# A hybrid decoder trunk on one core: the last 128 tokens leave the dense U products and take gathered rows

## The chip, the cores and the metric

The kernel runs on one core of one Trainium2 chip. Its engines are TensorE (PE, with its weight loads PEld), VectorE (DVE), ScalarE (ACT), GpSimd (POOL) and SyncE (SP), which issues transfers. The metric is the device time of one launch in microseconds. Everything is computed in float32; a product of two float32 matrices is made of three TensorE passes on rounded parts: hi x hi, hi x lo and lo x hi, where lo = raw - hi.

## The reference

512 tokens of width 1024 go through two layers. A layer mixes tokens in three ways (stick-breaking attention, a short convolution, a trailing-window pool), gates and projects the result, and then calls the retrieval feed-forward, which is what the change is about:

```python
q = xn @ w_query                       # 8 heads, two halves of 128
scores = q . sub_keys                  # per head and half: 128 scores
half_vals, half_idx = top_k(scores, 16)
cand = half_vals[0][:, None] + half_vals[1][None, :]      # 256 pairs
top_vals, top_pos = top_k(cand, 16)    # 16 of them per head: 128 experts per token
gates = softmax(top_vals)
u = take(expert_u, idx)                # rows of 1024 numbers
act = gelu(u . x_t) * gates
out = act . take(expert_v, idx)
```

There are 16384 experts (128 x 128). A last step adds a gated projection of a per-layer embedding (PLE).

## The kernel before

All weights come in one stream of tiles (128 partitions x 1024 numbers, 512 KB), in the order in which they are used. A ring of 8 buffers holds them. SP loads tile k+8 when tile k is done (`load`, L313). ACT rounds a tile to `hi` four tiles ahead (`split`, L442), and DVE or GpSimd then writes `lo` (DVE L766, GpSimd L389). A layer has 32 mixer tiles in four pairs of heads, 24 gate tiles, 12 branch tiles, 8 output tiles, 16 query tiles, 128 U tiles, 128 V tiles and 12 PLE tiles. In the mixers, gates, branches, outputs and queries DVE makes every `lo`; in the U stage GpSimd makes the first 96 after the start and DVE the rest; in the V stage DVE makes all.

**U stage.** For tile e, TensorE computes the 128 experts of that tile against all 512 tokens: 8 chunks x 3 passes, 24 matmuls of 128x512 (`dense`, L1182). ACT applies gelu (L592) and issues the store of the result to a table in DRAM, `early` (L595). Meanwhile DVE runs `select(c)` for the 128 tokens of block c (L985 to L1022): top 16 of each half, candidate sums, top 16 of these, indices and gates. TensorE turns the result of each select (`turn_slots`), after the numbers of tiles given in TURNS. Blocks 0 to 2 (384 tokens) get a dense gate table: for four tokens at a time (a quad), DVE builds one-hot matrices `RB` (L1040) and `LB` (L1045), TensorE multiplies them (L1377), ACT copies the product to `stage` (L625) and stores it. Two quads go into each of 48 U tiles; `hot_ready` tells TensorE that a quad is built, `hot_used` tells DVE that a buffer is free. Block 3, the tail, is selected afterwards; its tokens get index tables instead.

**V stage.** For the 384 tokens a group of four tiles is multiplied as activation x gate (`af`, L1076, split into `ah` by ACT and `al` by DVE, L1083), 18 matmuls of 128x512 a tile (L1397). For the tail GpSimd gathers, for each of its 128 slots, one activation cell per token out of `early` (L401, `hval`) and one V row of 4 KB per token (L409, `vrow`, four buffers); DVE multiplies hval by the gate (L1093) and adds the scaled row to `acc` (L1098).

Every engine works through its own instruction list in program order; a wait holds all that stands behind it. The interleaving is written out by hand on each engine.

The functions that the change touches, and what calls them:

## Time and profile before

| | |
|---|---|
| median of 3 runs | 4000.57 us (3999.61 to 4000.61) |
| profiled execution | 3998.72 us, span 3997.0 us |
| TensorE matmul busy | 3917.8 us, 98% of the span |
| TensorE weight loads | 3231.7 us, 81% |
| DVE | 2695.9 us, 67% |
| ACT | 1459.3 us, 37% |
| GpSimd | 1299.7 us, 33% |
| mean granted TensorE clock | 0.993 |
| DMA | 740.33 MB, mean 185 GB/s |

The two layers look alike in the trace. In the first, the mixers up to the end of the queries run to 611 us, the U stage from 611 to 1396 us, the V stage to 1929 us, and the PLE step to about 2010 us. Busy time says how much of the span an engine was occupied; what holds a stage must be read from the waits and the chain in that stage. A matmul's record is longer than its share of the time, since matmuls are pipelined: the distance between two starts is what it costs.

### The profile page before, as it was taken

How to read it: one execution, taken by the hardware profiler on the slowest of the kernel's cores; microseconds unless marked ns; L12 is line 12 of the kernel's file. 1: busy time of each engine (PE TensorE's matmuls, PEld its weight loads, DVE VectorE, ACT ScalarE, POOL GpSimd, SP SyncE). 2: the span in 40 equal slices, each digit the busy share in tenths (PEclk: the TensorE clock that was granted, in tenths of full speed). 3: DMA queues.
4: the chain of work that ended last, by engine and by line, in shares of the span. 5: the costliest groups of instructions: out<-in, count | busy, mean ns of one | idle time of the engine just before them, and what ended most of it. 6: DMA issues, size and time to landing. Idle time of an engine off the chain costs nothing.

```text
span 3997.0 us, 57322 instructions
## 1 busy us (share of the span) xinstructions
PE 3917.8 (98%) x18154; PEld 3231.7 (81%) x18154; DVE 2695.9 (67%) x4417; ACT 1459.3 (37%) x1925; POOL 1299.7 (33%) x887
## 2 busy tenths in 40 slices
PE   8999999999999999999999999999999999999997
PEld 5777888888888878888777778888888888788886
DVE  6753639967774277878677546498777732878785
ACT  5443333333333233333454333333333333333334
POOL 1100003433331076767201000044333401767661
PEclk9999999999999999999999999999999999999999
DMA  3222224445454699999322223244555546999992
GB/s 117 74 84 89 95 90 130 144 160 188 171 189 142 194 336 353 356 350 342 127 71 77 85 90 106 74 143 143 174 173 189 174 142 213 343 351 361 348 333 90
DMA packets 323763, 740.33 MB, mean 185 GB/s; under 512 B 30497, under 2 KB 161697, under 8 KB 319905
## 3 DMA queue, kind: packets, MB, share of 16 engines
q1 hardware_dynamic: 104400, 381.73, 29.6%
q10 hardware_dynamic: 174160, 222.40, 15.8%
q0 software_dynamic: 45056, 134.38, 9.1%
q8 instruction: 76, 1.25, 0.1%
q14 instruction: 71, 0.57, 0.1%
HBM read 618.87 MB, written 119.54 MB: 185 GB/s over the span
## 4 chain that ended last, share of the span: by engine, by line
PE 94%; DVE 2%; issue 1%; DMA 1%; ACT 1%; POOL 0%; DVEq 0%; ACTq 0%; POOLq 0%; SPq 0%
PE bank L1182 60%; PE bank L1397 25%; PE bank L1377 4%; PE bank L1244 1%; PE bank L1234 1%; PE bank L1252 1%; DVE xl L778 0%; DMA keyraw<-in_keys 0%; DMA vrow<-in_stream,tail_v 0%; PE bank L1327 0%; PE bank L1326 0%; ACT hi L442 0%; PE bank L1325 0%; PE bank L1229 0%; DMA early<-eo 0%
## 5 line engine op out<-in xcount | busy, mean ns | idle before, releaser
L1182 PE MATMUL bank<-xh,hi 128*128 128x512 f32 x3264 | 1305.9, 400 | 24.6 <-DVE xl L778 18.8
L1182 PE MATMUL bank<-xh,lo 128*128 128x512 f32 x3264 | 1273.9, 390 | 0.0
L1182 PE MATMUL bank<-xl,hi 128*128 128x512 f32 x3264 | 1273.8, 390 | 0.0
L766 DVE TENSOR_TENSOR lo<-raw,hi 128x1024 fp32r<-128x1024 f32 (+1 forms) x532 | 645.6, 1214 | 526.8 <-ACT hi L442 525.3
L442 ACT ACTIVATE hi<-raw 128x1024 fp32r<-128x1024 f32 x724 | 745.4, 1044 | 458.9 <-DMA raw<-in_stream 339.8
L389 POOL TENSOR_TENSOR lo<-raw,hi 128x1024 fp32r<-128x1024 f32 x192 | 478.5, 2492 | 979.8 <-ACT hi L442 979.5
L1182 PEld LDWEIGHTS bank<-xh,hi 128*128 128x128 f32 x3264 | 614.6, 188 | 160.9 <-DVE xl L778 23.8
L1182 PEld LDWEIGHTS bank<-xh,lo 128*128 128x128 f32 x3264 | 614.1, 188 | 130.2
L1182 PEld LDWEIGHTS bank<-xl,hi 128*128 128x128 f32 x3264 | 615.2, 188 | 122.9 <-issue 5.3
L401 POOL DMA_INDIRECT hval<-early,tail_h x256 | 384.8, 1503 | 431.5 <-PE bank L1397 351.2
L1397 PE MATMUL bank<-hi,ah 128*128 128x512 f32 x1536 | 475.6, 391 | 16.7 <-DVE al L1083 15.2
L1397 PE MATMUL bank<-lo,ah 128*128 128x512 f32 x1536 | 474.6, 390 | 0.0
L1397 PE MATMUL bank<-hi,al 128*128 128x512 f32 x1536 | 474.6, 390 | 0.0
L592 ACT ACTIVATE eo<-bank 128x512 f32<-128x512 f32 x256 | 153.2, 598 | 788.3 <-PE bank L1182 761.3
L1045 DVE TENSOR_SCALAR LB<-iota,tabs 128x128 f32<-128x128 f32 x768 | 418.2, 603 | 0.0
L409 POOL DMA_INDIRECT vrow<-in_stream,tail_v x256 | 322.7, 1261 | 225.3 <-DVE acc L1098 158.9
L1098 DVE SCALAR_TENSOR_TENSOR acc<-vrow,aval,acc 128x1024 f32<-128x1024 f32 x256 | 330.6, 1291 | 49.1 <-DMA vrow<-in_stream,tail_v 31.8
L1397 PEld LDWEIGHTS bank<-hi,ah 128*128 128x128 f32 x1536 | 289.6, 189 | 78.3 <-issue 18.3
L1397 PEld LDWEIGHTS bank<-lo,ah 128*128 128x128 f32 x1536 | 289.5, 188 | 60.4
L1397 PEld LDWEIGHTS bank<-hi,al 128*128 128x128 f32 x1536 | 289.5, 188 | 60.2
L1040 DVE TENSOR_TENSOR RB<-iota,tabs 128x512 f32<-128x512 f32 x192 | 131.6, 686 | 184.9 <-PE bank L1377 183.7
L1377 PEld LDWEIGHTS bank<-LB,RB 128*128 128x128 f32 x1536 | 200.7, 191 | 14.9
(209 smaller groups left out, 3405.6 us busy)
## 6 DMA issues: line engine op xcount, KB each, us to landing
raw<-in_stream SPq DMA_DIRECT2D x724, 512.0 KB, 3.9
early<-eo ACTq DMA_DIRECT2D x256, 256.0 KB, 3.9
gate_table<-stage ACTq DMA_DIRECT2D x24, 2048.0 KB, 8.3
gb<-gate_table ACTq DMA_DIRECT2D x64, 768.0 KB, 10.8
eb<-early ACTq DMA_DIRECT2D x64, 768.0 KB, 15.5
hval<-early,tail_h POOLq DMA_INDIRECT x256
vrow<-in_stream,tail_v POOLq DMA_INDIRECT x256, 8.6
hT<-in_xT ACTq DMA_DIRECT2D x2, 1024.0 KB, 8.3
```

Of the source, the lines that this page charges most:

```text
L389: pool.tensor_tensor(lo[k % RING][:, :], raw[k % RING][:, :], hi[k % RING][:, :].bitcast(f32), ALU.subtract).then_inc(lo_split, 1)
L401: pool.indirect_dma_start(hval[:, q:q + 1], None, early_cells, bass.IndirectOffsetOnAxis(tail_h[:, q:q + 1], 0)).then_inc(h_in[q // 4 % 2] ...
L409: pool.indirect_dma_start(vrow[j % 4][:, :], None, stream_rows, bass.IndirectOffsetOnAxis(tail_v[:, j:j + 1], 0)).then_inc(vrow_in[j % 4], 16)
L442: act.activation(hi[k % RING][:, 0:w], raw[k % RING][:, 0:w], ACT.Copy).then_inc(hi_split, 1)
L592: act.activation(eo[:, k % 2, :], bank[4 + k % 2][:, :], ACT.Gelu_apprx_tanh).then_inc(act_evac, 1)
L766: dve.tensor_tensor(lo[k % RING][:, 0:w], raw[k % RING][:, 0:w], hi[k % RING][:, 0:w].bitcast(f32), ALU.subtract).then_inc(lo_split, 1)
L1040: dve.tensor_tensor(RB[:, u, :, :], iota[:, :].unsqueeze(1).to_broadcast([P, 4, NK]), tabs[:, 1, bass.ds(i * 8 + u * 4, 4)].unsqueeze(2).t ...
L1045: last = dve.tensor_scalar(LB[:, u, q, :], iota[:, :], tabs[:, 0, bass.ds(t, 1)], tabs[:, 2, bass.ds(t, 1)], ALU.is_equal, ALU.mult)
L1098: dve.scalar_tensor_tensor(acc[:, :], vrow[r][:, :], aval[:, z, r:r + 1], acc[:, :], ALU.mult, ALU.add).then_inc(axpy_done, 1)
L1182: ins = pe.matmul(out_ap, st[slot][:, a:a + P], mv, start=first and i == 0, stop=last and i == 2)
L1377: ins = pe.matmul(bank[6 + u][:, q * P:(q + 1) * P], RB[:, u, q, :], LB[:, u, q, :], start=True, stop=True)
L1397: ins = pe.matmul(bank[m * 2 + h][:, :], a[:, z, k, m * P:(m + 1) * P], w[s % RING][:, h * SEQ:(h + 1) * SEQ], start=first and k == 0 and ...
```

## The change

The dense U products, their gelu and the table `early` now cover tokens 0 to 383 only (384 columns for 512). For the tail, U rows are gathered and multiplied with the tokens on DVE.

- **A row copy of expert_u.** U tiles hold experts in columns. During the mixers, gates, branches, outputs and queries of each layer SP loads each of the 128 U tiles into `turn_in` (two buffers), DVE transposes it in blocks of 32x32 into `turn_out` (`turn_rows`, two buffers), and SP stores it with four transfers into the DRAM table `rows_u` (pieces of 1 KB). SP waits for the transpose (`row_turned`) before it issues the next load and the stores; the turn waits for its load and for the stores of the turn two before. Turns per section: 10 for each pair of heads (8 tiles), 10 for each 8 gate tiles, 16 for the branches, 12 for the outputs, 30 for the queries.
- **Splits.** All `lo` parts up to the end of the U stage are made by GpSimd.
- **Order of the selects.** The tail (block 3) is selected first, then blocks 0 to 2. TensorE turns the slots of blocks 0 to 2 before tiles 33, 51 and 69. The table quads lie in tiles 72 to 119 (before: 36 to 83).
- **Dots.** ACT makes `x_tail`, the tail's tokens in the order of the copied rows, after tile 18. GpSimd gathers 128 rows of 4 KB per slot into `row` (four buffers), DVE multiplies and sums over 1024 numbers with one instruction per slot (`dots`). 10, 15 and 15 dots lie inside the three selects, 10 behind them, 60 between the quads, 18 at the end. ACT applies gelu to the 128 results at once.
- **Quads.** `LB` is built for four tokens with two instructions of 128x512 (compare, multiply) instead of four of 128x128.
- **V stage.** `aval` is made once; the gathers of single cells are gone. The V rows use the same four buffers.

GpSimd's list in the U stage, and the schedule of the gathers:

```python
DOTS = ((20, 0), (31, 10), (50, 26), (68, 42), (72, 50), (120, 110), (128, 128))

def dots_by(t):
    for (t0, n0), (t1, n1) in zip(DOTS, DOTS[1:]):
        if t0 <= t < t1:
            return n0 + (n1 - n0) * (t - t0) // (t1 - t0)
    return 0 if t < DOTS[0][0] else SLOTS

def gather(g, table, index):
    if g >= 4:
        pool.wait_ge(row_used, l * (2 * SLOTS) + (g - 2))
    apart(pool)
    pool.indirect_dma_start(row[g % 4][:, :], None, table,
                            bass.IndirectOffsetOnAxis(index, 0)).then_inc(row_in[g % 4], 16)

for e in range(NK):
    if e + AHEAD < NK:
        split(N_U + e + AHEAD)
    if e == DOTS[0][0] - 2:
        pool.wait_ge(tail_ready, l + 1)
        for z in range(2):
            pool.wait_ge(turn_stored[z], 64 + (l + 1) * (NK * 32))
    while e >= DOTS[0][0] - 2 and g < min(SLOTS, dots_by(e) + 3):
        gather(g, rows_u, tail_u[:, g:g + 1])
        g += 1
for j in range(SLOTS):
    gather(SLOTS + j, stream_rows, tail_v[:, j:j + 1])
```

DVE's list in the U stage:

```python
def dots(first, n):
    for j in range(first, first + n):
        dve.wait_ge(row_in[j % 4], l * (SLOTS * 8) + (j // 4 * 16 + 16))
        dve.tensor_tensor_reduce(row[j % 4][:, :], row[j % 4][:, :], x_tail[:, :], 1.0, 0.0,
                                 ALU.mult, ALU.add, hval[:, j:j + 1]).then_inc(row_used, 1)

select(MT)                       # then tail_v, tail_u, tail_g
dve.wait_ge(xt_ready, (l + 1) * 2)
select(0, 0, 5, 1)               # first dot, pauses to skip, one dot at each pause
select(1, 10, 0, 1)
select(2, 25, 0, 1)
take_tabs(MT - 1)
dots(40, 10)
dot = 50
for n in range(QUADS):
    u, four = n % 2, [P, 4, NK]
    dve.wait_ge(hot_used, l * QUADS + n + 1)
    link(dve.tensor_tensor(LB[:, u, :, :], iota..., column(0), ALU.is_equal))
    dve.tensor_tensor(RB[:, u, :, :], iota..., column(1), ALU.is_equal)
    dve.tensor_tensor(LB[:, u, :, :], LB[:, u, :, :], column(2), ALU.mult).then_inc(hot_ready, 1)
    if n % 2:
        more = 2 if n % 8 == 7 else 1
        dots(dot, more)
        dot += more
```

SP and DVE in the mixers:

```python
def store_rows(l, e):
    sp.wait_ge(row_turned, l * NK + (e + 1))
    if e + 2 < NK:
        fetch_u(l, e + 2)
    for b in range(4):
        sp.dma_start(rows_u[e * P:(e + 1) * P, b * 256:(b + 1) * 256].rearrange("(g j) n -> j g n", j=32),
                     turn_out[e % 2][b * 32:(b + 1) * 32, :].rearrange("j (g n) -> j g n", n=256))\
          .then_inc(turn_stored[e % 2], 16)

for k in range(N_U + 12):
    sp.wait_ge(tile_done, l * T + (k + 1))
    sp.dma_start(raw[k % RING][:, :], stream[...]).then_inc(raw_in[k % RING], 16)
    while done < NK and row_tile(done) + ROW_LEAD <= k:      # ROW_LEAD = 6
        store_rows(l, done)
        done += 1

def turn_rows(l, e, i=0, per=0):
    dve.wait_ge(turn_loaded[e % 2], l * (NK * 8) + i * (per * 8) + (e // 2 * 16 + 16))
    dve.wait_ge(turn_stored[e % 2], l * (NK * 32) + i * (per * 32) + (e // 2 * 64 + 64))
    dve.transpose(turn_out[e % 2]..., turn_in[e % 2]...).then_inc(row_turned, 1)
```

and in the dense products:

```diff
-                        dense(l, N_U + k, bank[4 + k % 2][:, :], (xh, xl), i, (xl_ready, l * (4 * DC) + 2 * DC) if k == 0 else None)
+                        dense(l, N_U + k, bank[4 + k % 2][:, 0:M], (xh[:, :, 0:M], xl[:, :, 0:M]), i,
+                              (xl_ready, l * (4 * DC) + 2 * DC) if k == 0 else None)
```

## Rows read from the trace of the kernel before

**Rows 1.** The chain that ended last, shares of the span by line.

```profile
PE bank L1182 60%; PE bank L1397 25%; PE bank L1377 4%; PE bank L1244 1%; PE bank L1234 1%; PE bank L1252 1%; DVE xl L778 0%; DMA keyraw<-in_keys 0%; DMA vrow<-in_stream,tail_v 0%; PE bank L1327 0%; PE bank L1326 0%; ACT hi L442 0%; PE bank L1325 0%; PE bank L1229 0%; DMA early<-eo 0%
```

**Rows 2.** Stages: length, busy PE, PEld, DVE, ACT, POOL, clock, DMA share, GB/s.

```profile
499.00:611.00 112.00, 111.16 (x582) 94.04 (x581) 48.17 (x54) 42.00 (x60) 0.00 (x0) 1.00 0.27 90
611.00:808.00 197.00, 197.00 (x875) 163.09 (x875) 178.49 (x635) 64.90 (x81) 91.40 (x35) 1.00 0.48 141
808.00:1153.00 345.00, 345.00 (x1905) 299.41 (x1905) 258.07 (x470) 126.82 (x191) 114.59 (x48) 1.00 0.52 177
...
1396.00:1929.00 533.00, 525.07 (x2303) 434.38 (x2304) 414.93 (x352) 177.97 (x161) 355.06 (x256) 0.99 0.96 338
```

**Rows 3.** The chain in order of time: start, length, count; 24 gate tiles.

```profile
252.53 130.80 PE bank L1182 x576
```

**Rows 4.** Timeline of TensorE in the attention: start, length of one.

```profile
116.84 0.34 PE L1244 MATMUL bank<-attSh,ones_r 128*128 128x384 f32 x1
117.02 0.35 PE L1244 MATMUL bank<-attSl,ones_r 128*128 128x384 f32 x1
```

**Rows 5.** Timeline of TensorE in the table phase.

```profile
891.48 1.05 PE L1377 MATMUL bank<-LB,RB 128*128 128x128 f32 x8
...
892.60 0.40 PE L1182 MATMUL bank<-xl,hi 128*128 128x512 f32 x1
```

**Rows 6.** Timeline of DVE in select(0).

```profile
611.96 3.19 DVE L985 MAX8 hv<-SC 128x8 f32<-128x128 f32 x16 [0.55 <-ACT SC L558]
...
656.02 2.29 DVE L1016 TENSOR_TENSOR eqi<-eqi,hxf 128x2048 f32<-128x2048 f32 x1
...
662.99 4.37 DVE L1016 TENSOR_TENSOR eqj<-eqj,hxf 128x2048 f32<-128x2048 f32 x1
...
670.58 3.19 DVE L985 MAX8 hv<-SC 128x8 f32<-128x128 f32 x16
```

**Rows 7.** Timeline of GpSimd beside it.

```profile
661.98 3.22 POOL L389 TENSOR_TENSOR lo<-raw,hi 128x1024 fp32r<-128x1024 f32 x1 [1.42 <-ACT hi L442]
```

**Rows 8.** A group of the page: out<-in, count, busy us, mean ns, idle before.

```profile
L1098 DVE SCALAR_TENSOR_TENSOR acc<-vrow,aval,acc 128x1024 f32<-128x1024 f32 x256 | 330.6, 1291 | 49.1 <-DMA vrow<-in_stream,tail_v 31.8
```

**Rows 9.** Timeline of ACT behind the last U tile.

```profile
1395.78 0.60 ACT L592 ACTIVATE eo<-bank 128x512 f32<-128x512 f32 x1 [3.82 <-PE bank L1182]
1396.27 1.05 ACT L442 ACTIVATE hi<-raw 128x1024 fp32r<-128x1024 f32 x1
```

**Rows 10.** Timeline of GpSimd in the table phase.

```profile
860.74 2.38 POOL L389 TENSOR_TENSOR lo<-raw,hi 128x1024 fp32r<-128x1024 f32 x1 [4.95 <-ACT hi L442]
```

**Rows 11.** Timeline of GpSimd in the V stage.

```profile
1459.30 0.95 POOL L409 DMA_INDIRECT vrow<-in_stream,tail_v  x1 [0.30 <-issue]
```

**Rows 12.** The tile vrow: its transfers.

```profile
DMA to landing us min/median/max: 4.6/8.6/11.2
```

**Rows 13.** The tile raw, 1420 to 1900 us (V stage).

```profile
DMA to landing us min/median/max: 3.8/6.3/8.5
```

**Rows 14.** The tile raw, 240 to 600 us: issue in ns, landing.

```profile
L313 SPq DMA_DIRECT2D raw<-in_stream x61: 332/333/338, 241.5 to 594.5; - x61
...
DMA to landing us min/median/max: 3.0/3.3/4.6
```

**Rows 15.** Timeline of DVE in the table phase.

```profile
860.66 3.31 DVE L1045 TENSOR_SCALAR LB<-iota,tabs 128x128 f32<-128x128 f32 x4
863.89 0.68 DVE L1040 TENSOR_TENSOR RB<-iota,tabs 128x512 f32<-128x512 f32 x1
864.49 1.11 DVE L1045 TENSOR_SCALAR LB<-iota,tabs 128x128 f32<-128x128 f32 x4
```

**Rows 16.** Timeline of TensorE at the start of the V stage.

```profile
1420.56 1.22 PE L1397 MATMUL bank<-hi,ah 128*128 128x512 f32 x2 [7.43 <-DVE al L1083]
1421.57 1.06 PE L1397 MATMUL bank<-lo,ah 128*128 128x512 f32 x2
...
1426.47 0.62 PE L1397 MATMUL bank<-lo,ah 128*128 128x512 f32 x2
```

More of the change, by code:

```diff
@@ L612, in _ @@
                         if e == after:
-                            exponents(c)
+                            exponents(n, (n + MT) % NBLK)
+                    if e == DOTS[0][0] - 2:
+                        act.wait_ge(tail_ready, l + 1)
+                        act.wait_ge(xt_turned, l + 1)
+                        for z in range(2):
+                            act.activation(x_tail[:, :].rearrange("p (b c q) -> p c b q", b=4, c=DC)[:, z * 4:z * 4 + 4],
+                                           bank[6 + z][:, :].rearrange("p (c b q) -> p c b q", c=4, b=4), ACT.Copy)\
+                               .then_inc(xt_ready, 1)
@@ L918, in _ @@
                         if m % 2:
-                            split(l, N_BR + k + AHEAD)
+                            for n in range(R0_BR, R0_OUT):
+                                if row_tile(n) == N_BR + k:
+                                    turn_rows(l, n)
                         if j == 0 and m == 1:
@@ L957, in _ @@
                         low_xn(DC - 1)
-                    split(l, N_QRY + k + AHEAD)
+                    for n in range(R0_QRY, NK):
+                        if row_tile(n) == N_QRY + k:
+                            turn_rows(l, n)
                     if k == 2:
```

369 lines of the change are left out of this document (213 added, 156 removed).

## The prediction

> **What bounds the kernel now.** The profiled execution took 3998.7 us for a span of 3997.0 us; the median of the runs is 4000.6 us. I work in the profiled execution's time; the 1.9 us to the median are half a tenth of a per cent, under what a measurement of this kernel can tell from no change (0.2%, 8 us). The chain of waits comes first: 60% of it is the dense line and 25% the value line, all TensorE [rows 1]. The table of stages says the same: TensorE is busy without a gap in the U stage (611 to 1396 us in the first layer, 785.3 us), DMA at 0.5 there and at 0.96 in the value stage [rows 2]. So only fewer TensorE columns can shorten it, as long as nothing else becomes the bound.
>
> **What is removed.** A U tile is 24 matmuls. At 512 columns 576 of them take 130.8 us, 227 ns each [rows 3]. At 384 columns two starts lie 0.18 us apart [rows 4]; 227 less a quarter of 512 columns (53 ns) is 174 ns, which I take: 4.18 us a tile for 5.45. The 48 tiles that carry the gate tables also hold two groups of table matmuls each, 1.12 - 0.23 = 0.89 us a group [rows 5], hence 5.97 us for 7.24. By TensorE alone the stage is 80 x 4.18 + 48 x 5.97 = 621 us, 164 us less in a layer. The question is whether the others can follow.
>
> **The selection phase (tiles 0 to 71).** A select takes 670.6 - 612.0 = 58.6 us now [rows 6]; I take 61, since GpSimd's splits come every 4.2 instead of 5.4 us and collide: a DVE multiply of 2.29 us took 4.37 [rows 6] because a GpSimd split had begun just before it, and that split had itself waited for a DVE pass (3.22 us for 2.4) [rows 7]. A dot over 1024 elements is like the acc update, 1.29 us [rows 8], 1.2 us apart; with a collision now and then I take 1.9 us, between 1.2 (none) and 3.5 (all). From the U stage's start at 0: the tail's select and its table of rows end at 65 us. The DVE then waits for x_tail, which ACT makes after tile 18, at 83 us. select(0) with 10 dots ends at 163 (TensorE wants its slots before tile 33, at 138 plus 7 us lost to the exponents, and waits 18 us), select(1) with 15 dots at 252, select(2) at 342 (tile 69). Dots 40 to 49 follow; dot 49's row is asked for only after tile 71, done at 354. First table quad ready: 367 us. If a dot costs 1.2, 340.
>
> **The table phase (tiles 72 to 119).** Here an order written out by hand decides. GpSimd handles tile e+4's split after ACT has rounded it, which is after tile e is done, and only then issues the gathers up to dots_by(e)+2. dots_by rises by 5 in 4 tiles from 50 at tile 72, so the iteration of tile 72+k reaches gather 52 + (5k)//4. The DVE builds quads 2m and 2m+1 for tile 72+m, then does dot 50+m+(m+1)//4, then quad 2m+2, without which tile 73+m cannot start. For every odd m that gather belongs to the iteration of tile 71+m: m=1 wants 51 (k=0), m=3 wants 54 (k=2), m=5 wants 56 (k=4). The lead of three gathers is used up. The loop is:
> - tile 71+m done to its rounding done: 0.2 + 0.4 + 1.05 = 1.65 us [rows 9], the gelu shortened for 384 columns;
> - GpSimd split 2.39, then 0.3 to the gather [rows 10, 11];
> - gather from issue to landing: in the value stage 4.6 at least, 8.6 median [rows 12]. Direct loads there took 6.3, in the mixers 3.3 [rows 13, 14]. DMA here will be about as in the same phase now, half busy [rows 2], so I take 5.0; bounds 3.3 (a direct load's) and 8.6;
> - dot 1.2, quad (three passes of 512 at 0.6 to 0.7) 1.95 [rows 15];
> - tile 73+m on TensorE 5.97.
> Sum 18.5 us for two tiles, of which TensorE works 11.9 and idles 6.6. After an idle of 7.4 us 14 matmuls of 512 columns took 5.91 us, where 14 x 0.227 = 3.2 is the rule: the lower clock level, 2.7 us lost [rows 16]; I take 1.7, between 0 and 2.7. So 20.2 us for two tiles, 10.1 a tile. The first tiles ride on what was gathered before; tile 74 starts at 386, tile 120 at 386 + 46 x 10.1 = 850.
>
> **The port.** DVE and GpSimd exclude each other for whole instructions in these rows: four LB passes took 3.31 us beside a split and 1.11 without it [rows 10, 15]. That is how a tile would cost 3.9 (quads) + 1.25 x 1.2 (dots) + 2.1 (split) = 7.5 us if nothing else held; inside 10.1 us it fits into the DVE's wait. The Trainium skill (SBUF — State Buffer, "SBUF: two separate sides") states it as a lock held for a whole instruction and names DVE instructions with two SBUF inputs; the change turns one-input LB passes into such ones and puts all splits on GpSimd, so the rule speaks against it, and the trace agrees (2.29 to 4.37 us). What it gives as a result of its own is the second rival.
>
> **The end of the stage.** Tiles 120 to 127 need 33 us. Dots 110 to 127 need gathers of the iterations up to 123 (done 17 us in), then 9 more gathers, each waiting for a dot four before: the last dot 44 us in, then low(0), 47 us. U stage 850 + 47 = 897 for 785.3: **+112 us a layer**. With landing 3.3 and no clock loss a tile is 8.4: +34. With 8.6 and 2.7 it is 12.5: +222. The Trainium skill (DMA: Bandwidth & Descriptors, "Anatomy of one DMA") fits a GpSimd-issued transfer as 2.0 us plus its bytes at 436 GB/s, an estimate of 3.2 us for 512 KB; by it the sum would come out some 80 us lower. The least that the trace shows is 4.6 [rows 12], so the trace does not agree.
>
> **Mixers and queries.** DVE: 92 splits go, 128 turns come. No row shows a turn; a pass over 1024 elements in the DVE costs 1.29 [rows 8], I take 1.2 between 0.6 (half) and 2.4 (twice). DVE was busy 48 of 112 us in the query stage [rows 2] and 30 turns for 16 splits add 17: hidden. GpSimd takes the splits, 2.4 us of every 5.4 [rows 10, 3] with four tiles of lead: hidden. DMA is the matter: each turn loads and stores 0.52 MB. Query stage: 16 tiles and 30 turns are 39.8 MB in 112 us, 356 GB/s, where the value stage got 338 at a share of 0.96 [rows 2]: +6 us. Likewise the output stage (16.8 MB in 44 us) +6 and the branch stage (23.1 MB in 65 us) +3. Besides, a turn waits for the store of the one two before: issue 5 x 0.33 [rows 14] and landing 3.3 to 6.3 [rows 13, 14] make a turn every 3.1 to 4.6 us, and the query stage wants one every 3.6. What waits behind a held turn on DVE is the next bank's evacuation, and behind it TensorE; on SP, which waits for the turn, the next tile load, which has two tiles of slack. I take +25 a layer, between 0 and 60. At the kernel's start two U loads stand ahead of the first tile: +3 once.
>
> **Value stage.** The 256 gathers of single cells go, and with them the late aval that held the second group: TensorE waited 7.4 us for al [rows 16]. -7.4 a layer. It stays TensorE's: 128 tiles x 18 x 0.227 = 523 of 533 us. Layer entry on SP waits for the last acc update, which ends before the loads are wanted: 0.
>
> **Sum.** 2 x (25 + 112 - 7.4) + 3 = +262: 3998.7 + 262 = **4261 us**, slower by 6.5%. Its own range is 4060 to 4430: 4055 with all low ends; all high ends give 4550, which I cut since the 8.6 us landing belongs to full queues.
>
> **Rivals.**
> - *TensorE keeps the pace* (faster). The gathers lie far enough ahead after all, the DVE never holds a quad. Decides when landing + dot + quad fit in TensorE's own two tiles (L + 3.2 below 5.97 for the odd ones). Dots at 1.2: first quad at 323, tables 287, end 41: 651 us, -134 a layer; 3998.7 + 2 x (25 - 134 - 7.4) + 3 = 3769. For: the DVE is idle a quarter of the table phase now [rows 2]. Against: the loop's rows. 0.13.
> - *The port or the DVE bounds the table phase*: 7.5 us a tile, 367 + 360 + 47 = 774, -11 a layer: 4015. For it: the collisions in [rows 6, 7, 10, 15]. Against: it needs a landing under 3 us or a gather issued an iteration earlier than I read. 0.15.
> - *The row copy is dearer*: turns at 4.6 us and more from branch to queries, +80 a layer for +25, on top of the forecast: 4371. For: DMA wanted over 338 GB/s. Against: the first half of the mixers leaves room. 0.13.
> - The forecast 0.56; others, such as turns far dearer than 2.4 us, 0.03.
>
> Faster by over 0.2% takes the first rival and some of the second: 0.17. Within 0.2%: 0.03. Slower 0.80. The range 3970 to 4430 leaves out the first rival and a few hundredths at each end.
>
> **What would show it.** After: 384-column matmuls 174 ns apart in plain stretches; TensorE waits in the table phase charged to RB or LB on DVE, some 6 us every second tile, and the DVE's to row gathers; clock under 1 there; table phase near 485 us a layer. Selection phase ending near 367 with waits for slots before tiles 33, 51 and 69. DMA share near 1 in queries. Value stage shorter by 7. I am wrong if tiles 72 to 119 come at 6 us (first rival) or at 7.5 with the DVE never idle (second).

## The result and the profile after

The changed kernel takes 4462.3 us (median of 4 runs, 4457.7 to 4469.8) where the kernel before, beside it, takes 4000.6 (3999.6 to 4004.9): a ratio of 1.1154, 95% interval 1.1134 to 1.1173. It is slower by 11.5%. I had forecast slower, 4261 us, with a range from 3970 to 4430: the sign is right, the time lies outside the range. The profiled execution took 4460.3 us, 461.6 more than that of before, where the sum said 262.

The chain of waits of the kernel after, shares of the span by engine and then by line; [rows 1] had 60% on the dense line alone:

```profile
PE 34%; issue 27%; DVE 19%; DMA 10%; POOL 4%; SPq 4%; ACT 1%; DVEq 0%; POOLq 0%; ACTq 0%
PE bank L1544 24%; PE bank L1325 9%; DMA rows_u<-turn_out 8%; POOL row L505 4%; SPq L375 3%; DVE turn_out L873 3%; DVE row L1099 2%; DMA row<-rows_u,tail_u 1%; SPq L366 1%; DVE attS L942 1%; DVE BR L990 1%; DVE slot L1156 1%; DVE hx L1125 1%; DVE hx L1122 1%; DVE S L1123 1%
```

TensorE's share of the chain has fallen to 34%, most of it in the value stage (L1544); its dense line (L1325) holds 9%. The stores of the row copy (rows_u<-turn_out) are the largest newcomer. The stages of the first layer, columns as in [rows 2]: pairs of heads, gates, branches, outputs, queries, then the U stage in its selection phase, table phase and end, then the value stage:

```profile
0.00:277.30 277.30, 246.59 (x1039) 183.65 (x1040) 213.68 (x258) 126.49 (x217) 109.68 (x115) 0.98 0.70 226
277.30:417.20 139.90, 129.99 (x559) 106.26 (x558) 53.65 (x60) 47.80 (x61) 59.93 (x25) 0.97 0.99 332
417.20:505.40 88.20, 75.02 (x301) 59.56 (x301) 67.61 (x73) 19.17 (x24) 28.23 (x12) 0.93 0.81 261
505.40:564.60 59.20, 53.48 (x220) 42.05 (x219) 27.73 (x30) 21.12 (x28) 26.49 (x15) 0.96 0.94 313
564.60:693.70 129.10, 107.17 (x541) 90.16 (x542) 61.54 (x65) 37.66 (x54) 38.12 (x16) 0.92 0.94 305
693.70:1067.20 373.50, 312.09 (x1738) 310.20 (x1738) 337.98 (x945) 118.37 (x160) 264.43 (x123) 0.91 0.68 212
1067.20:1577.00 509.80, 346.66 (x1934) 335.85 (x1935) 289.68 (x403) 124.32 (x192) 187.82 (x107) 0.83 0.51 173
1577.00:1642.40 65.40, 33.24 (x180) 32.60 (x178) 32.78 (x43) 14.27 (x19) 35.24 (x27) 0.77 1.00 364
1642.40:2167.00 524.60, 524.49 (x2306) 434.24 (x2307) 408.92 (x323) 174.79 (x159) 196.47 (x125) 1.00 0.95 340
```

Gates, branches, outputs and queries of the kernel before, cut in the same way, at the first evacuation of each stage:

```profile
258.30:392.40 134.10, 129.65 (x565) 106.91 (x564) 48.42 (x52) 48.33 (x62) 0.00 (x0) 0.99 0.28 94
392.40:460.40 68.00, 68.00 (x301) 56.29 (x300) 49.76 (x68) 17.32 (x23) 0.00 (x0) 1.00 0.28 93
460.40:510.80 50.40, 50.40 (x221) 40.97 (x219) 22.15 (x25) 19.96 (x26) 8.38 (x6) 1.00 0.35 115
510.80:611.00 100.20, 99.36 (x534) 85.02 (x533) 43.91 (x51) 37.40 (x55) 0.00 (x0) 1.00 0.24 79
```

The nine stages against the sum (us, first layer):

| stage | before | after | difference | forecast |
|---|---|---|---|---|
| pairs of heads, with the start | 258.3 | 277.3 | +19.0 | |
| gates | 134.1 | 139.9 | +5.8 | |
| branches | 68.0 | 88.2 | +20.2 | |
| outputs | 50.4 | 59.2 | +8.8 | |
| queries, to the U stage | 100.2 | 129.1 | +28.9 | |
| mixers and queries together | 611.0 | 693.7 | **+82.7** | +28 |
| selection phase | | 373.5 | | 367 |
| table phase | | 509.8 | | 483 |
| end of the stage | | 65.4 | | 47 |
| U stage together | 785.3 | 948.7 | **+163.4** | +112 |
| value stage | 533.0 | 524.6 | -8.4 | -7.4 |

In the second layer the stretch from the value stage to the end of the queries takes 67 us more (731.4 for 664.5), the U stage 163 again. The sum is thus short by 55 and 42 us in the mixers and by 51 twice in the U stage, and long by 1 twice in the value stage: 197 of the 200 us that are missing.

**The U product.** Timeline of TensorE in the selection phase (start, length of one), to be held against [rows 4]:

```profile
800.85 0.33 PE L1325 MATMUL bank<-xh,lo 128*128 128x384 f32 x1
801.03 0.33 PE L1325 MATMUL bank<-xh,hi 128*128 128x384 f32 x1
801.20 0.33 PE L1325 MATMUL bank<-xl,hi 128*128 128x384 f32 x1
```

Two starts lie 0.17 to 0.18 us apart, the 174 ns taken.

**The table phase.** One round of the loop over two tiles, timeline of all engines without the dense product; the bracket gives the idle time before and what ended it:

```profile
1127.55 2.37 DVE L1099 CUSTOM_DVE_ANT_0 row<-row,x_tail 128x1024 f32<-128x1024 f32 x1 [6.95 <-DMA row<-rows_u,tail_u]
...
1129.85 0.68 DVE L1206 TENSOR_TENSOR LB<-iota,tabs 128x512 f32<-128x512 f32 x1
...
1131.18 0.68 DVE L1208 TENSOR_TENSOR LB<-LB,tabs 128x512 f32<-128x512 f32 x1
...
1131.92 2.08 PE L1527 MATMUL bank<-LB,RB 128*128 128x128 f32 x8 [6.96 <-DVE LB L1208]
...
1141.45 1.05 ACT L541 ACTIVATE hi<-raw 128x1024 fp32r<-128x1024 f32 x1
...
1142.58 2.38 POOL L453 TENSOR_TENSOR lo<-raw,hi 128x1024 fp32r<-128x1024 f32 x1 [11.83 <-ACT hi L541]
...
1145.11 0.95 POOL L505 DMA_INDIRECT row<-rows_u,tail_u  x1
...
1148.45 2.34 POOL L453 TENSOR_TENSOR lo<-raw,hi 128x1024 fp32r<-128x1024 f32 x1 [2.39 <-ACT hi L541]
1149.54 2.33 DVE L1099 CUSTOM_DVE_ANT_0 row<-row,x_tail 128x1024 f32<-128x1024 f32 x1 [7.49 <-DMA row<-rows_u,tail_u]
```

From dot to dot 22.0 us. TensorE starts the tile at 1131.92; ACT's rounding behind it ends at 1142.5, 10.6 us later: 1.65 from the tile's end to there as in [rows 9], which leaves 8.9 us for the tile (7.7 with the clock loss that I took; the granted clock is 0.50 for the first 6 us behind the idle time of 6.96 us, the lower of its two levels, 1.2 GHz for 2.4, and 1.00 from 1138 on). The split takes 2.4; the gather is issued 0.15 later and has landed 4.4 us after its issue; the dot takes 2.3 where it takes 1.22 alone, since GpSimd's next split (1148.45) runs beside it; the quad takes 1.95. The 24 rounds take 505 us, 21.0 on average. Of the phase's 59 dots in this view the 20 that had waited over 5 us for their row took 2.2 to 2.8 us, the other 39 took 1.2. The gathers of this phase land in

```profile
DMA to landing us min/median/max: 4.2/5.1/8.7
```

for the 5.0 that I took out of 3.3 to 8.6 [rows 12 to 14]. TensorE's idle of 6.96 us every second tile is the 6.6 of the sum, and its mean granted clock is 0.83 in the phase.

**The end of the U stage.** The last dot ends 63.6 us after tile 120 begins, where the sum had 44. Two rows of ACT (its queue, then its next gelu):

```profile
1596.34 7.78 ACTq L744 DMA_DIRECT2D eb<-early  x1
1604.29 0.49 ACT L691 ACTIVATE eo<-bank 128x384 f32<-128x384 f32 x1 [13.68 <-issue]
```

ACT issues two fetches of tables behind one another, and its gelu comes 13.7 us late. TensorE waits 9.3 us for that gelu, GpSimd's split 7.4 us for the rounding behind it, and between 1598.4 and 1608.6 GpSimd issues no gather.

**The row copy.** The tile turn_out in the query stage, by line: duration in ns (min, median, max), first and last start; then who waited, and from issue to landing:

```profile
L375 SPq DMA_DIRECT2D rows_u<-turn_out x120: 303/456/1507, 567.0 to 687.5; - x120
L873 DVE STREAM_TRANSPOSE turn_out<-turn_in x30: 1205/1245/1248, 565.2 to 684.6; 128x1024 f32<-128x1024 f32 x30
  DMA rows_u<-turn_out: 64.8, 27
DMA to landing us min/median/max: 2.0/4.1/6.4
```

The turn costs what I took (1.24 for 1.2). But 27 of 30 turns wait for the stores of the turn two before, 64.8 us in 130. Two turns from the same buffer, VectorE and SyncE's queue:

```profile
605.80 1.25 DVE L873 STREAM_TRANSPOSE turn_out<-turn_in 128x1024 f32<-128x1024 f32 x1 [1.11 <-DMA rows_u<-turn_out]
...
607.54 0.36 SPq L366 DMA_DIRECT2D turn_in<-in_stream  x1
607.95 2.96 SPq L375 DMA_DIRECT2D rows_u<-turn_out  x4
...
613.86 1.25 DVE L873 STREAM_TRANSPOSE turn_out<-turn_in 128x1024 f32<-128x1024 f32 x1 [2.20 <-DMA rows_u<-turn_out]
```

8.1 us for two turns here; over the stage two turns take 8.3 us at the median (7.0 to 10.9), and the 30 turns come 4.1 us apart on average. Behind a held turn stand ql and the branch evacuation; TensorE waited 23.5 us for ql alone.

### The profile page after: what moved, and what is told of

Its sections match the earlier page's. It is cut to its first block, busy times and chain, and to the rows that moved or that the text cites. A ratio compares the mean times of both kernels' runs of the same rounds, so it can differ in the third digit from the quotient of the medians.

```text
span 4458.6 us, 59328 instructions
## 1 busy us (share of the span) xinstructions
PE 3775.5 (85%) x18170; PEld 3282.3 (74%) x18170; DVE 3084.3 (69%) x4497; ACT 1442.7 (32%) x1931; POOL 1911.9 (43%) x1127
## 3 DMA queue, kind: packets, MB, share of 16 engines
q10 hardware_dynamic: 149584, 205.63, 12.9%
## 4 chain that ended last, share of the span: by engine, by line
PE 34%; issue 27%; DVE 19%; DMA 10%; POOL 4%; SPq 4%; ACT 1%; DVEq 0%; POOLq 0%; ACTq 0%
PE bank L1544 24%; PE bank L1325 9%; DMA rows_u<-turn_out 8%; POOL row L505 4%; SPq L375 3%; DVE turn_out L873 3%; DVE row L1099 2%; DMA row<-rows_u,tail_u 1%; SPq L366 1%; DVE attS L942 1%; DVE BR L990 1%; DVE slot L1156 1%; DVE hx L1125 1%; DVE hx L1122 1%; DVE S L1123 1%
## 5 line engine op out<-in xcount | busy, mean ns | idle before, releaser
L453 POOL TENSOR_TENSOR lo<-raw,hi 128x1024 fp32r<-128x1024 f32 x432 | 1083.9, 2512 | 1395.7 <-ACT hi L541 1393.9
L1325 PE MATMUL bank<-xh,hi 128*128 128x384 f32 (+1 forms) x3264 | 1240.8, 380 | 86.1 <-ACT eo L691 37.4
L1325 PE MATMUL bank<-xl,hi 128*128 128x384 f32 (+1 forms) x3264 | 1199.0, 367 | 0.0
L1325 PE MATMUL bank<-xh,lo 128*128 128x384 f32 (+1 forms) x3264 | 1195.7, 366 | 0.0
L1099 DVE CUSTOM_DVE_ANT_0 row<-row,x_tail 128x1024 f32<-128x1024 f32 x256 | 444.2, 1739 | 484.4 <-DMA row<-rows_u,tail_u 472.4
L1325 PEld LDWEIGHTS bank<-xh,hi 128*128 128x128 f32 x3264 | 648.3, 199 | 155.7 <-issue 78.7
L1325 PEld LDWEIGHTS bank<-xl,hi 128*128 128x128 f32 x3264 | 646.1, 198 | 51.6 <-issue 5.8
L1325 PEld LDWEIGHTS bank<-xh,lo 128*128 128x128 f32 x3264 | 642.2, 197 | 51.5
L505 POOL DMA_INDIRECT row<-in_stream,tail_v x256 | 394.3, 1540 | 630.0 <-DVE acc L1238 607.6
L873 DVE STREAM_TRANSPOSE turn_out<-turn_in 128x1024 f32<-128x1024 f32 x256 | 317.1, 1241 | 340.3 <-DMA rows_u<-turn_out 339.9
L866 DVE TENSOR_TENSOR lo<-raw,hi 128x1024 fp32r<-128x1024 f32 x292 | 359.4, 1231 | 231.6 <-ACT hi L541 231.5
L1544 PE MATMUL bank<-hi,ah 128*128 128x512 f32 x1536 | 475.0, 390 | 45.6 <-DVE al L1226 45.6
L1544 PE MATMUL bank<-lo,ah 128*128 128x512 f32 x1536 | 474.4, 390 | 0.0
L1544 PE MATMUL bank<-hi,al 128*128 128x512 f32 x1536 | 473.9, 390 | 0.0
L505 POOL DMA_INDIRECT row<-rows_u,tail_u x256 | 327.5, 1279 | 138.3 <-DVE hval L1099 99.8
L1544 PEld LDWEIGHTS bank<-hi,ah 128*128 128x128 f32 x1536 | 289.2, 188 | 106.2 <-issue 46.2
L1238 DVE SCALAR_TENSOR_TENSOR acc<-row,aval,acc 128x1024 f32<-128x1024 f32 x256 | 327.9, 1281 | 8.9 <-DMA row<-in_stream,tail_v 8.6
L1544 PEld LDWEIGHTS bank<-lo,ah 128*128 128x128 f32 x1536 | 289.5, 188 | 60.3
```

Source lines behind the costliest of these rows:

```text
L453: pool.tensor_tensor(lo[k % RING][:, 0:w], raw[k % RING][:, 0:w], hi[k % RING][:, 0:w].bitcast(f32), ALU.subtract).then_inc(lo_split, 1)
L505: pool.indirect_dma_start(row[g % 4][:, :], None, table, bass.IndirectOffsetOnAxis(index, 0)).then_inc(row_in[g % 4], 16)
L866: dve.tensor_tensor(lo[k % RING][:, 0:w], raw[k % RING][:, 0:w], hi[k % RING][:, 0:w].bitcast(f32), ALU.subtract).then_inc(lo_split, 1)
L873: dve.transpose(turn_out[e % 2][:, :].rearrange("p (g c q) -> p c g q", g=4, c=DC), turn_in[e % 2][:, :].rearrange("p (c g q) -> p c g q", ...
L1099: dve.tensor_tensor_reduce(row[j % 4][:, :], row[j % 4][:, :], x_tail[:, :], 1.0, 0.0, ALU.mult, ALU.add, hval[:, j:j + 1]).then_inc(row_u ...
L1238: dve.scalar_tensor_tensor(acc[:, :], row[r][:, :], aval[:, bass.ds(i * 8 + z * 4 + r, 1)], acc[:, :], ALU.mult, ALU.add).then_inc(row_use ...
```

## The experiments

Each is told by its change against the kernel named; times are single runs beside the kernel before (4000.3 to 4003.3) unless an interval stands. Four runs of one kernel with the copy lie up to 19 us apart (copy_fetch_late, 4034.2 to 4052.9; after, 4457.7 to 4469.8), so a difference of single runs under some 20 us says little.

### The row copy

**no_copy** (against after): no loads into turn_in, no turns, no stores.

> The kernel after without the row copy: the 128 loads into turn_in, the turns on VectorE and the stores into rows_u of each layer are left out, and the gathers of the dots take other rows of the stream in their place (same number, same 4 KB rows), so its output is not the reference's. Theory (the row copy was mis-sized in my prediction: +82 us a layer for +25): the U stage starts at 611 to 616 us instead of 694, and the kernel takes about 4460 - 2 x 80 = 4300 us. Rival (the mixers are held by the lo splits that went to GpSimd): the U stage still starts after 670 us and the kernel stays above 4410 us.

Measured 4329.7: the copy costs 130 to 133 us (against 4460.3 and 4462.3), 65 a layer. The U stage starts at 624, not at 611 to 616: some 12 us a layer remain of the mixers' loss with no copy at all.

**copy_unheld** (against after):

```diff
-                                 turn_out[e % 2][b * 32:(b + 1) * 32, :].rearrange("j (g n) -> j g n", n=256))\
+                                 consts[b * 32:(b + 1) * 32, :].unsqueeze(1).to_broadcast([32, 4, 256]))\
...
-                dve.wait_ge(turn_stored[e % 2], ...)
```

> The kernel after, but the four stores of each turn read a buffer of constants (ident and ones) instead of turn_out, so the turn no longer waits for the stores of the turn two before. Loads, turns, stores, bytes, piece sizes and queues are the same; what lands in rows_u is not expert_u, so the output is not the reference's. Theory (a loop of turn, issue and landing of four stores holds VectorE, some 8.3 us for two turns in the queries): most of the 82 us go; the U stage starts at 620 to 645 us and the kernel takes about 4340 us (4310 to 4375). Rival (the bandwidth of the DMA engines is full, share 0.94 to 0.99 in gates, outputs and queries): the start stays at 675 us or later and the kernel above 4420 us.

4402.1, and the U stage starts at 660, both between the two: the loop of the two buffers is worth 58 us, 29 a layer. Now the turns wait for their loads:

```profile
DVE turn_out L872 <- DMA turn_in<-in_stream: 82.2, 47, 4.0
```

(engine, what it waited for: us in total, times, longest; up to 640 us). Both theories hold a part.

**one_store_in_four** (against after): `for b in range(1)` for `range(4)` in the stores, semaphore counts to match.

> The kernel after with one of the four stores of each turn left (32 of 128 partitions); the dots' gathers take other rows of the stream, so the output is not the reference's. All loads and turns stay; bytes stored and store issues are a quarter, and a loop of two turns (1.25 + 0.3 + 0.4 + 0.5 + 4 us) is no longer than two turns are wanted apart. no_copy took 4330, copy_unheld 4402, the kernel after 4460. Theory (what the copy costs beside the loop, 36 us a layer, is the DMA engines' bandwidth, which the loads alone do not fill): 4350 us (4335 to 4365). Rival (it is the turns' time on VectorE and the loads on SyncE ahead of the tiles): 4385 us or more.

4365.0, right at the edge of the theory's range. By differences of runs the copy's 130 us (both layers) fall into three: 35 remain with loads, turns and a quarter of the stores; 37 more come with the other three quarters of the stores as traffic and issues (copy_unheld less this); 58 with VectorE waiting for them. The parts are not clean: here VectorE still waited 28.9 us in the first layer for the one store, and in copy_unheld it waited for loads instead. So the 35 are not shown to be bandwidth.

**turns_even** (against lead_one_more, below): 12, 10, 14, 12 and 24 turns for 10, 10, 16, 12 and 30. The two more in a pair stand behind the ninth and tenth, at its end.

> lead_one_more with the turns spread more evenly over the mixers: 12 for each pair of heads (for 10), 10 for each 8 gate tiles, 14 for the branches (for 16), 12 for the outputs, 24 for the queries (for 30). The same copy, the same output. Theory (a turn costs 4.15 us wherever VectorE meets them closer than that; the query stage of 98 us has room for 23 or 24, not for 30): the query stage falls from 126 to 100 to 105 us, the branches by 3 to 6 us, the pairs lengthen by at most 10 us: 4192 - 2 x 20 = 4150 us (4130 to 4175). Rival (each turn costs TensorE its share wherever it stands, because the copy's 133 MB a layer share the DMA engines with the tiles): the sum of the stages stays within 8 us and the kernel at 4180 us or more.

4234.9 for 4192.3: slower by 43, a miss. The queries fell from 125.3 to 106.4 us between their first and last ql, and the branches from 86.2 to 80.2, as expected; the pairs of the first layer grew by 47. VectorE in the pairs, turns_even and then lead_one_more (waits up to the gates):

```profile
DVE turn_out L873 <- DMA rows_u<-turn_out: 51.2, 18, 4.9
```

```profile
DVE turn_out L873 <- DMA rows_u<-turn_out: 11.9, 9, 2.8
```

Twelve turns fit into a pair by the average, but four in a row at its end don't, and behind them stands the evacuation for which TensorE's next tiles wait. I read from this that the distance between neighbours counts; a run with the twelve spread inside the pair, which would show it, was not made.

**stores_by_g** (against splits_on_dve, below):

```diff
-                for b in range(4):
-                    sp.dma_start(rows_u[e * P:(e + 1) * P, b * 256:(b + 1) * 256]..."(g j) n -> j g n",
-                                 turn_out[e % 2][b * 32:(b + 1) * 32, :]...)
+                for g in range(4):
+                    sp.dma_start(rows_u[e * P + g * 32:e * P + (g + 1) * 32, :].rearrange("j (b n) -> b j n", b=4),
+                                 turn_out[e % 2][:, g * 256:(g + 1) * 256])
```

> splits_on_dve with the four stores of a turn cut the other way: each takes 256 columns of all 128 partitions (128 pieces of 1 KB) where each took all 1024 columns of 32 partitions (also 128 pieces of 1 KB). Same bytes, pieces, queue and number of transfers. Theory (the loop of two turns, 8.3 us, is mostly stores: issue 2.0 and landing 4.1 us; reading all partitions at once makes a transfer land sooner): the mixers up to the end of the queries take 690 us now and 665 to 682 then, 4066 - 2 x 16 = 4034 us (4015 to 4055). Rival (issue and landing don't depend on the partitions read): the mixers within 5 us of 690 and the kernel within 10 us of 4066.

4734.0 for 4066.4, much slower: neither theory. SyncE's queue after a turn, in this kernel:

```profile
607.72 0.33 SPq L366 DMA_DIRECT2D turn_in<-in_stream  x1
608.10 5.46 SPq L375 DMA_DIRECT2D rows_u<-turn_out  x4
613.84 1.65 SPq L386 DMA_DIRECT2D raw<-in_stream  x1
```

Four stores of the same bytes and the same 1 KB pieces take 5.5 us to issue for 2.0 to 3.0, and the tile load behind them 1.65 for 0.36. The loop is longer by that much: VectorE waits 512 us for stores before the first layer's U stage. Between 600 and 638 us SyncE's queue is never free for more than 0.7 us, so there its issuing is the bound.

### The table phase and the end of the U stage

**lead_one_more** (against after), one constant:

```diff
-                    while e >= DOTS[0][0] - 2 and g < min(SLOTS, dots_by(e) + 3):
+                    while e >= DOTS[0][0] - 2 and g < min(SLOTS, dots_by(e) + 4):
```

> The kernel after with one constant changed: GpSimd issues the gathers up to dots_by(e)+3 instead of dots_by(e)+2 in the iteration of tile e. Theory (the loop of rounding, split, gather, landing, dot and quad sets 10.7 us a tile in the table phase): the gather leaves up to one iteration earlier, the loop opens, and the table phase falls from 516 us a layer to 360 to 420 us (7.5 to 8.7 us a tile, then VectorE and GpSimd on the shared port): 4460 - 2 x 125 = 4210 us (4150 to 4280). Rival (VectorE and GpSimd work without a gap at the port, the gather is not what holds): the table phase stays above 490 us and the kernel above 4410 us.

4192.3, as the loop's theory has it: 270 us for one constant. The table matmuls run over 361 us in place of 505, 7.5 us a tile. That is the pace that my second rival gave for a phase in which the port decides. Stages 1070 to 1435 us of this kernel:

```profile
1070.00:1435.00 365.00, 311.58 (x1929) 292.96 (x1930) 339.06 (x406) 124.00 (x192) 213.74 (x106) 0.97 0.71 241
```

VectorE is busy for 339 of 365 us, the clock back at 0.97. 19 of the phase's 60 dots took 1.8 to 3.4 us; each of them overlapped a split on GpSimd and ended 1.07 to 1.09 us behind that split's end, as if it had begun only then.

**dots_unheld** (against after): the 60 dots of the phase read x_tail twice, wait for no row and write to a spare buffer; GpSimd waits for its own gathers in their place.

> The kernel after, but the 60 dots between the quads multiply x_tail with itself and do not wait for their gathered row (product into a spare buffer); GpSimd waits for its own gather of four before instead, so all gathers, dots, splits and quads are still done and only the tie from a landing to VectorE is cut. Output not the reference's. Theory (the tie is what holds the table phase): 516 us a layer fall to 340 to 380 us, 7.1 to 7.9 us a tile, what the port lets through; the kernel takes about 4460 - 2 x 155 = 4150 us. Rival (it is VectorE's and GpSimd's work at the shared port that fills 10.7 us a tile): no less than 490 us, the kernel above 4410 us.

4158.5: 354 us for the phase. With every tie to the landing cut the phase is 7 us shorter than with one gather of lead, so that one gather was nearly all that was missing there. The kernel is 34 us shorter than lead_one_more; the two table phases account for 15 of them.

**splits_on_dve** (against lead_one_more): the lo splits of tiles 75 to 122 stand behind the dots on VectorE.

```diff
+                        split(l, N_U + HOT_E + 3 + n // 2)      # VectorE, behind the dots of tile 72 + n//2
```

> lead_one_more with the 48 lo splits of the tiles 75 to 122 of each layer moved from GpSimd to VectorE, one behind the dots of each tile. Theory (in the table phase VectorE and GpSimd share the port and exclude each other: quads 3.9 + dots 1.5 + GpSimd's split 2.1 = 7.6 us a tile): a split on VectorE takes 1.2 us where GpSimd's shut VectorE out for some 2.2, so a tile takes 6.6 to 6.8 us and the table phase 320 us for 361: 4192 - 2 x 42 = 4108 us (4080 to 4140). Rival (VectorE's own work is the bound, the port no part of it): 48 x 1.2 = 58 us more work for VectorE a layer, the table phase 400 us or more and the kernel above 4250 us.

4066.4, 126 us less than lead_one_more, more than expected; 110 of them lie in the two table phases (306 us each, first to last table matmul, for 361). The phase:

```profile
1070.00:1380.00 310.00, 298.15 (x1926) 287.07 (x1927) 305.54 (x457) 121.81 (x192) 71.01 (x58) 0.99 0.82 284
```

48 splits more on VectorE, and it is busy for 34 us less: a split on GpSimd cost VectorE more than the split itself costs it (2.4 to 2.7 us of exclusion for 1.23). A tile takes 6.4 us, VectorE working 305.5 of 310. The Trainium skill (SBUF — State Buffer, "SBUF: two separate sides") calls it an exclusive lock for a whole instruction, and the trace of lead_one_more agrees (the 19 dots above).

**lb_of_four** (against lead_one_more): LB by four passes of 128x128, as before the change.

> lead_one_more with LB built as in the kernel before: four tensor_scalar passes of 128x128 (compare and multiply at once, 0.28 us each) for the two passes of 128x512 (0.69 us each). One part of the change undone. Theory (VectorE's and the port's time sum up in the table phase): 0.27 us less for a quad, two quads a tile, 0.5 us a tile: the table phase 361 to 337 us, 4192 - 2 x 25 = 4142 us. Rival (the four passes lose to GpSimd's split what they save, as 3.31 us for four beside a split before): unchanged within 10 us or slower.

4211.5, slower by 19; the rival. Timelines of VectorE and, in the second fence, of GpSimd:

```profile
1200.50 3.13 DVE L1209 TENSOR_SCALAR LB<-iota,tabs 128x128 f32<-128x128 f32 x4
...
1204.15 1.10 DVE L1209 TENSOR_SCALAR LB<-iota,tabs 128x128 f32<-128x128 f32 x4
```

```profile
1201.10 2.45 POOL L453 TENSOR_TENSOR lo<-raw,hi 128x1024 fp32r<-128x1024 f32 x1 [2.92 <-ACT hi L541]
```

The four passes take 1.10 us alone (two of 512: 1.37) and 3.13 beside the split. So passes with one input are shut out too, as in [rows 15], and the step from one-input to two-input passes, which the prediction held against the change, cost nothing here. The 19 us are within what single runs can differ by, but the table phase is longer in both layers: 386 and 367 us, for 361 twice. Why it is slower, not equal, I leave open.

**end_and_x_tail** (against splits_on_dve): low(0,0) ahead of dots 120 to 127, the splits of V tiles 1 to 3 ahead of the last dots, ACT's fetches later, x_tail after tile 16.

> splits_on_dve with the order at two places changed, all work the same: low(0,0) before the dots 120 to 127 (it stood behind dot 127), ACT's first two fetches of tables one tile and three tiles later, and x_tail made after tile 16 for 18. Theory (each is a wait of an in-order engine for work that it does not need): the end of the U stage 63 to 45 to 52 us, the selection phase 377 to 368 to 371 us: 4066 - 2 x 21 = 4024 us (4005 to 4045). Rival (the last dots, late behind low(0,0), hold the splits of the first V tiles, and TensorE waits for these): what is won at the end is lost at V tiles 1 to 4, and the kernel stays above 4050 us.

4039.0: 27 us for the 42 expected. VectorE's wait for x_tail fell from 14.0 to 5.7 us. At the end TensorE now waits for another piece of VectorE's work, and ACT stands still for 14.6 us: its second fetch takes 13.4 us to issue, and 1.2 us after that issue lands the store whose buffer the next gelu needs (two views: waits; timeline of ACT):

```profile
PE bank L1552 <- DVE lo L870: 20.0, 1, 20.0
```

```profile
1401.22 13.41 ACTq L747 DMA_DIRECT2D eb<-early  x1
1415.82 0.49 ACT L694 ACTIVATE eo<-bank 128x384 f32<-128x384 f32 x1 [14.55 <-DMA early<-eo]
```

**all_orders** (end_and_x_tail with stores_by_g):

> end_and_x_tail and stores_by_g together: the change with the row copy still in it and every reordering tried so far that should help. Theory: the gains stand in different stages and add up: 4066 - 42 - 32 = 3992 us (3970 to 4030), about the kernel before. Rival (the row copy, 70 us a layer, cannot be hidden by order): 4025 us or more, slower than before.

4698.6, ratio 1.1748 (1.1729 to 1.1768): it carries stores_by_g's loss and says nothing more.

**copy_best_order** (against end_and_x_tail): the split of V tile 0 ahead of low(0,0).

> end_and_x_tail with the split of V tile 0 ahead of low(0,0) and of the dots 120 to 123 (in end_and_x_tail TensorE waited 20.0 us for it, 7.5 of them behind these dots). Theory: 2 x 7.5 us off 4039: 4024 us (4012 to 4034), still slower than the kernel before: the row copy is not paid back. Rival (ACT's fetch, whose issue took 13.4 us and held the gelu of tile 125, ends last anyway): 4035 us or more.

4038.5, ratio 1.0091 (1.0075 to 1.0106): no gain, as the rival has it. Here TensorE, done with the last U tile, waits for its gelu (first layer, waits from 1340 to 1500 us):

```profile
PE bank L1552 <- ACT eo L694: 15.0, 1, 15.0
```

**copy_fetch_late** (against copy_best_order): the second and third fetch behind the last gelu.

> copy_best_order with ACT's second and third fetch of tables behind the gelu of the last U tile (they stood behind the tiles 125 and 126). Theory (in copy_best_order the issue of the second fetch took 13.6 us on ACT's queue with the DMA engines full, the gelu of tile 126 and 127 came behind it, and TensorE waited 15.0 us for that gelu before the value stage): TensorE then waits for al alone, ready some 8 us sooner: 4038 - 2 x 8 = 4022 us (4010 to 4030). Rival (the fetches late, the second value group comes too late and TensorE waits there): 4036 us or more.

4043.1, ratio 1.0097 (1.0081 to 1.0112): no gain again. TensorE's first wait at the value stage fell (15.0 to 12.9 us in the first layer, 15.9 to 10.2 in the second), and its wait for the second group rose (7.2 to 8.5, 5.1 to 7.7), so the rival holds a part. The rest is that ACT's hold has changed its name: in the first layer the gelu of tile 126 now waits for its buffer, that is for the store of tile 124 into `early`, issued on the same queue behind the first fetch and landed some 19 us later:

```profile
1392.67 3.32 ACTq L747 DMA_DIRECT2D eb<-early  x1
...
1396.70 0.35 ACTq L697 DMA_DIRECT2D early<-eo  x1
1415.92 0.49 ACT L694 ACTIVATE eo<-bank 128x384 f32<-128x384 f32 x1 [14.86 <-DMA early<-eo]
```

So the issue time alone was not the cause. What I take from both traces, and have not tried by itself: a small transfer queued behind a fetch of tables on ACT's queue is late with it; neither of my two places for the fetches mended that. With the copy in it, every order that I found is slower than before, the best by 38 us.

### Without the copy, and the removed columns alone

**before_narrow**: the kernel before with 384 columns in its U products.

> The kernel before with its U products cut to the first 384 columns (24 matmuls of 128x384 a tile); gelu, table, selects, tables and gathers of cells as before, so the last 128 tokens take stale values and the output is not the reference's. It prices the removed columns alone. My term: 53 us less per thousand matmuls, 24 x 128 x 0.053 = 163 us a layer, 3674 us if nothing else comes to bound it. The selects then end after tile 33 wants its slots (three selects are 176 us, tile 33 stands at 140), which I put at 20 to 37 us a layer: 3710 us (3680 to 3760). Rival (384 columns cost as much as 512 because weight loads bound the pitch): above 3850 us.

3792.3: 211 us less than before, not 290 or 326, and above the expected range (3680 to 3760). The table phase runs at the term (48 tiles in 283 us, 5.9 each, for 5.97), but TensorE waits for VectorE's slots and others:

```profile
PE bank L1353 <- DVE slot L1022: 64.9, 6, 11.5
```

The waits for slots are the 32 us a layer that I had expected. From 609 to 760 us, in the selection phase, its clock is 0.92. Removing columns from a full TensorE gave back two thirds of their price.

**rows_given** (against end_and_x_tail): no copy; the rows are a further input laid out by the host.

```diff
+    rows = a["expert_u"].reshape(DEPTH * NK * P, DC, 4, 32).transpose(0, 2, 1, 3).reshape(DEPTH * NK * P, D)
...
-                        gather(g, rows_u, tail_u[:, g:g + 1])
+                        gather(g, given_rows, tail_u[:, g:g + 1])
```

> end_and_x_tail without the row copy, and the dots' rows gathered from one more input: expert_u row by row, laid out by the host beside the tiles (64 MB a layer more in DRAM; two more DVE steps a layer for the layer's offset). Output that of the reference. Theory (the row copy costs 65 us a layer, as no_copy showed against the kernel after): 4024 - 130 = 3894 us (3870 to 3925), faster than before by 2.7%. Rival (the copy's cover is used by other waits once it is gone, among them the splits on GpSimd): above 3950 us.

3908.0, ratio 0.9778 (0.9762 to 0.9794): faster than before by 2.2%, and 131 us below end_and_x_tail, the price of the copy again.

**given_best_order** (copy_best_order's edit on it):

> The same order of the end with rows_given (rows of expert_u as one more input, no row copy). Theory: 3908 - 15 = 3893 us (3880 to 3902). Rival as for copy_best_order: 3903 us or more.

3906.6: nothing, as there.

**given_splits_back** (against given_best_order): the lo splits of the mixers on VectorE, as before the change.

> given_best_order with the lo splits of pairs, gates, branches, outputs and queries on VectorE, as in the kernel before (GpSimd makes those of the U tiles 4 to 74, VectorE those of 75 to 122). It prices the step that I cost at nothing. Theory (in no_copy the U stage began at 624 us for 611, with no turns left: GpSimd's splits stand in the way of its masks): 12 us a layer, 3893 - 24 = 3869 us (3855 to 3885), and the U stage begins at 611 us. Rival (those 12 us have another cause): 3888 us or more.

3884.1, ratio 0.9716 (0.9703 to 0.9729): 22.5 us less, 11 a layer, and the U stage begins at 612 us. It is the fastest version here with the right output, 2.8% faster than before, at the price of expert_u in DRAM twice.

**given_fetch_late** (copy_fetch_late's edit on it):

> The same edit on given_splits_back, where TensorE waited 29.4 us in two layers for the gelu at the same place. Theory: 8 to 12 us a layer, 3884 - 20 = 3864 us (3855 to 3874). Rival as for copy_fetch_late: 3882 us or more.

3887.7, ratio 0.9714 (0.9701 to 0.9727): no difference, as with the copy.

What is left, in given_splits_back's selection and table phases:

```profile
609.70:990.00 380.30, 321.63 (x1804) 317.82 (x1803) 356.76 (x962) 121.73 (x166) 260.28 (x126) 0.92 0.69 215
990.00:1300.00 310.00, 299.03 (x1940) 287.94 (x1939) 296.95 (x444) 123.85 (x194) 74.50 (x60) 1.00 0.84 289
```

The first holds TensorE to 322 of 380 us with VectorE busy for 357; the second has both full.

## Why the prediction missed the time, and what it had right

- **Removed columns: right.** 174 ns a matmul, measured 0.17 to 0.18 apart.
- **Selection phase: right**, 373.5 for 367, with slot waits of 36.9 us in the layer's three turns.
- **The loop in the table phase: right in kind, 5% short in size.** 510 us for 483. Landing 5.1 for 5.0, the lead used up as read from the lists; lead_one_more and dots_unheld show that this tie held the phase at its length. Two terms were small: the dot that closes the loop meets GpSimd's next split (2.2 to 2.8 us in 20 rounds of 24, for 1.2), and the tile at the lower clock costs 8.9, not 7.7, in the round shown. 27 us a layer.
- **The end of the stage: short.** 65 for 47. I had the gathers' chain alone. The fetches of tables fill the DMA engines there (share 1.00): gathers land in 8.0 us (median) against 5.1 in the phase before. And the issue of the fetches holds ACT for 13.7 us, by which GpSimd's gathers stop for 10 us. 18 us a layer; how they divide between the two, no run shows.
- **The step that failed: "I take +25 a layer, between 0 and 60", the mixers and queries.** The measured difference is 83 and 66. The mechanism stood in the text, a turn every 3.1 to 4.6 us for a want of 3.6; the size was wrong in three ways. The loop came out at 4.1 us a turn: a store's issue is 0.45 us at the median and up to 1.5, not the 0.33 of a plain load [rows 14], and I chose below the middle of my own bounds. The want was 3.3, not 3.6: the 112 us that I divided held the end of the outputs, and the 16 query evacuations of the kernel before lie within 98 us. And the costs that I had added lightly, 6 us of bandwidth for the queries and a few for the rest, and the turns' own time, which I called hidden, are 36 us a layer beside the loop by no_copy and copy_unheld. 65 us a layer in all.
- **"GpSimd takes the splits ...: hidden": wrong by 11 us a layer** (given_splits_back). I compared averages, 2.4 us of every 5.4. That GpSimd's masks are what the splits hold up was my theory; no run separates it.
- **Value stage: right**, -8.4 for -7.4.

Of the rivals, the dearer row copy (4371) had its price about right, 83 and 66 us a layer for 80, though at 4.1 us a turn and not its 4.6; on top of it the U stage was short by 51: 4261 + 55 + 42 + 2 x 51 - 2 = 4458. The mixers' 83 and 66 lie above even my high end of 60. The range ended at 4430 since I had cut the sum of all high ends, 4550, for the landing of 8.6 us in it; several other terms came out high together. The port rival had its number right (7.5 us a tile) for the kernel with one gather more of lead.

The Trainium skill (DMA: Bandwidth & Descriptors, "Anatomy of one DMA") fits 3.2 us for such a gather, an estimate, as the prediction said; the least of 58 in the table phase took 4.2, so the trace of the kernel after disagrees with it as well.

## What to carry to other kernels

A hand-over through two buffers has a period: work, issue and landing of one turn. Hold it against the closest distance at which the in-order engine meets it, not against the mean over a stage, and then add the traffic separately. Where an order is written out by hand, count the lead of each transfer in iterations against its landing: here one gather of lead was worth 270 us, more than half of the loss. And an engine that is "idle anyway" is no free place for work that shuts another one out: 48 splits of a layer were cheaper on the engine that bounds the phase.

## What the runs showed of the hardware

- The issue of a store on SyncE's queue depends on its form: 128 pieces of 1 KB out of 32 partitions took 0.45 us at the median, out of 128 partitions 1.12 (stores_by_g, first layer; 5.46 for four in the rows shown), and the plain tile loads behind them went from 0.36 to 1.65.
- A second fetch of 768 KB on ACT's queue took 13.4 us (end_and_x_tail) and 13.6 us (copy_best_order) to issue with the DMA share at 1.03; in copy_best_order ACT's next activation waited 13.7 us for that issue. With the fetch issued later, a 192 KB store behind the first fetch took some 19 us to land and held the activation 14.9 us (copy_fetch_late, first layer; 7.3 in the second).
- An instruction of VectorE that met a split of GpSimd waited for its end: 19 dots ended 1.07 to 1.09 us behind a split's end, whatever they took in all (lead_one_more).
- A block transpose (32x32) of 128x1024 float32 takes VectorE 1.24 us, as long as a `lo` split of the same size (1.23).
- Multiply and sum over 1024 numbers takes 1.22 us, and 0.08 to read the accumulator.
- TensorE's granted clock follows its idling: 0.83 over the table phase with 7 us of idle every second tile, 0.97 with one gather more of lead, 0.99 with the splits on VectorE.
